# Spreading steps of the routing weights: two behind every second expert block, in two pairs of PSUM banks, in place of one behind each block

## The reference, cut to what matters

```python
ids = e1 * PEER_N_KEYS + e2                       # 128 experts per token (8 heads x top 16)
wts = jax.nn.softmax(top_v, axis=-1)
...
ue = jnp.take(u, idx, axis=0)
act = jnp.einsum('td,tkd->tk', hx, ue)
coef = w * jax.nn.gelu(act, approximate=False)
ve = jnp.take(v, idx, axis=0)
return jnp.einsum('tk,tkd->td', coef, ve)
```

## Time and profile before

| what | value |
|---|---|
| time, median of 3 runs | 1499.66 us (1498.52 to 1499.95) |
| time of the profiled execution | 1499.56 us |
| its span | 1497.7 us |
| TensorE busy | 1476.2 us (99%) |
| VectorE busy | 1243.0 us (83%) |
| ScalarE busy | 577.9 us (39%) |
| GpSimd busy | 438.9 us (29%) |
| DMA, mean over the span | 289 GB/s |

### The profile page before, as it was taken

One profiled execution on the slowest core, in us unless ns is written; L12 is line 12 of the kernel. 1 busy time (PEld: TensorE's weight loads), 2 busy tenths in 40 slices (PEclk: granted clock), 3 DMA queues, 4 the chain that ended last, 5 costly groups with the idle time before them and its releaser, 6 DMA issues.

```text
span 1497.7 us, 21867 instructions
## 1 busy us (share of the span) xinstructions
PE 1476.2 (99%) x8153; PEld 1302.1 (87%) x8153; DVE 1243.0 (83%) x2368; ACT 577.9 (39%) x869; POOL 438.9 (29%) x373
## 2 busy tenths in 40 slices
PE   8999999999999999999999999999999999999998
PEld 4788878788999999999999999988888888888886
DVE  5687868776899997999999945698888888888886
ACT  4422244522333333444444443343333333333333
POOL 1120100010578986432222202222222222222210
PEclk9999999999999999999999999999999999999999
DMA  9772423234469896799999999999999999999983
GB/s 379 271 264 87 141 96 113 60 88 148 142 210 307 293 304 220 259 347 360 365 378 360 372 321 362 382 406 359 378 355 377 371 388 378 388 358 373 366 318 131
DMA packets 152215, 433.50 MB, mean 289 GB/s; under 512 B 13520, under 2 KB 46544, under 8 KB 150224
## 3 DMA queue, kind: packets, MB, share of 16 engines
q1 hardware_dynamic: 76352, 203.91, 37.4%
q0 software_dynamic: 42048, 153.11, 28.2%
q10 hardware_dynamic: 33744, 75.64, 13.5%
HBM read 378.08 MB, written 54.53 MB: 289 GB/s over the span
## 4 chain that ended last, share of the span: by engine, by line
PE 74%; DVE 19%; DMA 4%; issue 1%; ACT 1%; POOL 0%; SPq 0%; DVEq 0%; ACTq 0%
PE ps L1733 23%; PE ps L1735 22%; PE ps L1734 22%; PE ps L2137 3%; DVE rows L1530 2%; DMA g_dram<-g_buf 2%; DVE ps L1562 1%; DMA part_w<-w_ada 1%; DVE ps L1566 1%; DVE picks L1568 1%; PE ps L2077 1%; DMA ada_w<-w_ada 1%; DVE tv L1496 1%; DVE tv L1499 1%; DVE ti L1500 1%
## 5 line engine op out<-in xcount | busy, mean ns | idle before, releaser
L1733 PE MATMUL ps<-hT_hi,ws_hi 128*128 128x384 f32 (+1 forms) x976 | 341.3, 350 | 2.8 <-POOL ws_lo L652 1.6
L1735 PE MATMUL ps<-hT_hi,ws_lo 128*128 128x384 f32 (+1 forms) x976 | 335.3, 344 | 0.0
L1734 PE MATMUL ps<-hT_lo,ws_hi 128*128 128x384 f32 (+1 forms) x976 | 335.1, 343 | 0.0
L1733 PE MATMUL ps<-vs_hi,coef_hi 128*128 128x512 f32 x768 | 298.8, 389 | 1.7 <-DVE coef_lo L1692 1.7
L1735 PE MATMUL ps<-vs_hi,coef_lo 128*128 128x512 f32 x768 | 298.8, 389 | 0.0
L1734 PE MATMUL ps<-vs_lo,coef_hi 128*128 128x512 f32 x768 | 298.8, 389 | 0.0
L994 ACT ACTIVATE vs_hi<-blk_raw 128x1024 fp32r<-128x1024 f32 x128 | 135.7, 1060 | 284.7 <-PE ps L1735 282.6
L660 POOL DMA_INDIRECT rows<-u_nat,ids x128 | 143.7, 1122 | 299.9 <-DVE sp_act L1530 292.0
L660 POOL DMA_INDIRECT rows<-v_nat,ids x128 | 127.1, 993 | 332.9 <-DVE ps L1650 298.5
L1689 DVE TENSOR_TENSOR vs_lo<-blk_raw,vs_hi 128x1024 fp32r<-128x1024 f32 x128 | 156.7, 1224 | 67.3 <-ACT vs_hi L994 65.4
L940 ACT ACTIVATE ws_hi<-blk_raw 128x1024 fp32r<-128x1024 f32 x102 | 108.1, 1060 | 239.7 <-PE ps L1735 225.4
(11 more groups left out here) (322 smaller groups left out, 2226.7 us busy)
## 6 DMA issues: line engine op xcount, KB each, us to landing
blk_raw<-u_t SPq DMA_DIRECT2D x128, 512.0 KB
blk_raw<-v_nat SPq DMA_DIRECT2D x128, 512.0 KB
g_dram<-g_buf ACTq DMA_DIRECT2D x128, 192.0 KB
w_dram<-w_stage SPq DMA_DIRECT2D x48, 512.0 KB
grp_g<-g_dram ACTq DMA_DIRECT2D x15, 1536.0 KB
grp_w<-w_dram ACTq DMA_DIRECT2D x15, 1536.0 KB
part_w<-w_ada POOLq DMA_DIRECT2D x24, 512.0 KB, 5.9
raw<-w_in SPq DMA_DIRECT2D x20, 512.0 KB, 5.9
```

The source lines that it names most:

```text
L1733: pe.matmul(o, lh, rh, start=start, stop=False, skip_group_check=True)
L1734: pe.matmul(o, lh, rl, start=False, stop=False, skip_group_check=True)
L1735: return pe.matmul(o, ll, rh, start=False, stop=stop, skip_group_check=True)
```

## The change

TensorE's steps come in pairs. Behind the products of every odd block of the stage it runs `spread(q, 0)` and `spread(q + 1, 1)`; behind an even block it runs none. The even step writes banks 2 and 3, the odd one banks 4 and 5. ScalarE copies both steps behind the odd block (`pair_after`). VectorE's order stays: one-hots of one step in each block. The blocks without one-hots are now the last two of each 16 (66, 67, 82, 83, 98 and 99) in place of the last of each 8, and with them move the bursts of three rows and the blocks in which SyncE issues no store. `PART_END` stays 106.

```diff
-PART_END = PART_A + STEPS // 7 * 8 + STEPS % 7
+PART_END = PART_A + STEPS // 14 * 16 + STEPS % 14
 def spreads_after(b):
-    if not PART_A <= b < PART_END or (b - PART_A) % 8 == 7:
+    if not PART_A <= b < PART_END or (b - PART_A) % 16 >= 14:
         return None
-    return (b - PART_A) // 8 * 7 + (b - PART_A) % 8
+    return (b - PART_A) // 16 * 14 + (b - PART_A) % 16
+
+def pair_after(b):
+    q = spreads_after(b)
+    return () if q is None or q % 2 == 0 else (q - 1, q)
...
-                    src = ps[:, 2 + r, :].rearrange("p (t b) -> p b t", t=4)
+                    src = ps[:, 2 + 2 * (q % 2) + r, :].rearrange("p (t b) -> p b t", t=4)
...
-                if spreads_after(b) is not None:
-                    take_w(spreads_after(b))
+                for q in pair_after(b):
+                    take_w(q)
...
-                    o = ps[:, 2 + t // 4, (t % 4) * P:(t % 4 + 1) * P]
+                    o = ps[:, 2 + 2 * p + t // 4, (t % 4) * P:(t % 4 + 1) * P]
...
-                if j % 8 < 7:
-                    spread(q, q0(j) % 2, free)
+                if j % 2 and j % 16 < 14:
+                    spread(q, 0, free)
+                    spread(q + 1, 1, None if free is None else free + 2)
 
             def q0(j):
-                return j // 8 * 7 + j % 8
+                return j // 16 * 14 + j % 16 - 1
 
             for j in range(16):
-                part(j, PART_A + j, q0(j), 2 * q0(j) if q0(j) else None)
+                part(j, PART_A + j, q0(j), 2 * (q0(j) - 1) if q0(j) > 0 else None)
             with pe.Fori(1, STEPS // 14) as i:
                 for j in range(16):
-                    part(j, 16 * i + (PART_A + j), 14 * i + q0(j), 28 * i + 2 * q0(j))
+                    part(j, 16 * i + (PART_A + j), 14 * i + q0(j), 28 * i + 2 * (q0(j) - 1))
             for j in range(STEPS // 14 * 16, PART_END - PART_A):
-                part(j, PART_A + j, q0(j), 2 * q0(j))
+                part(j, PART_A + j, q0(j), 2 * (q0(j) - 1))
```

## The result

| | before | after |
|---|---|---|
| median of 8 runs | 1498.62 us (1498.32 to 1499.95) | 1502.76 us (1501.86 to 1504.75) |
| ratio, 95% interval | | 1.0027 [1.0018, 1.0036] |
| profiled execution, its span | 1499.56, 1497.7 us | 1504.64, 1502.8 us |

The 8 runs of before contain the 3 of the table further up.

What follows compares the result with a forecast made beforehand. The prediction took TensorE to set the time, busy 40.00 of 40 us, with VectorE having little air. It summed -2.4 - 0.52 + 0.51 + 0.53 + 1.1 = -0.8 us on 1499.56, giving 1498.8 us, range 1497.2 to 1502.5.

Steps and rivals of the forecast that it cites:

- 24 switches: TensorE's switches from steps back to products: 24 of 48 go at 0.10 us each, -2.4 us.
- first wait, start: TensorE's wait at the first step goes, -0.52 us; late low parts at blocks 54 and 55 add +0.51 and +0.53.
- new wait at 19 pairs: VectorE's one-hots wait for the pair's first step, making TensorE 0.06 us late at 19 pairs: +1.1 us.
- three doubled bursts: Six gathered rows in two neighbouring blocks, three times: the gather is there in time, cost taken as 0.
- the one issued at 721.41: A gather on GpSimd's queue, said to land within 6.6 us, from four gathers' 2.06 MB moved between 718 and 728 us.
- T: Start of a pair of steps on TensorE, after an odd block; the forecast's times count from it.
- the fourth: Rival: at 10 us landing, doubled bursts make the low part 2 us late three times, +6, 1504.8 us; chance 0.08.
- harmless by itself: VectorE's idle time at the new wait, forecast some 20 times at about 0.8 us.
- TensorE's 0.97 us per step: Price of one step with its switch on TensorE: 16 matmuls 0.87 us, switch back to products 0.10.
- the stretch without one: TensorE around block 59, which has no step: 9.29 us against 5.13, so a bare block takes 4.16 us.
- the loads explain the switch: TensorE's 0.10 us switch put down to a 188 ns fp32r weight load with only a 0.054 us matmul to hide under.
- The stall: TensorE late at `products(b+1)` behind a pair: second matmul at T + 6.24 against T + 6.18, 0.06 us.

Runs made afterwards that it cites:

- e3: Kernel before with single steps, no pairing; only the blocks without a step moved together, giving bursts of six rows: 1499.48 us, ratio 1.0.
- a2: The changed kernel run again unedited, as the mark for its group: 1502.28 us, ratio 1.0025 against the kernel before.
- e5: Changed kernel with VectorE's row ahead of the one-hots in one block of 16, the last before a burst: 1498.47 us, ratio 1.0003.
- e8b: Changed kernel with three quarters of the `w_stage` stores taken out of the stage; part of the result wrong: 1531.57 us in one run, stage 261.16 us.
- e6: e2 with one gathered row each taken from blocks 52 and 53 and put to 106 and 110: 1495.19 us, ratio 0.9973 against the kernel before.
- e1: Changed kernel with one row in place of three in each burst's second block, six rows moved behind block 114: 1500.43 us, ratio 1.0009.
- e2: Changed kernel with VectorE's row put ahead of the one-hots in even blocks: 1497.52 us, ratio 0.999 against the kernel before.
- e7: Changed kernel with both steps of a pair in banks 2 and 3, the odd one waiting for ScalarE's copy: 1576.91 us in one run.
- e6b: e6 run again unedited, as the mark for its group: 1494.64 us, ratio 0.9968 against the kernel before.

## Why the prediction was wrong, by its own steps

| term | forecast | measured |
|---|---|---|
| 24 switches | -2.4 | 24 x 0.08 = -1.9 |
| first wait, start | -0.52 + 1.04 | -0.52 + 1.03 |
| new wait at 19 pairs | +1.1 | 19 x 0.03 = +0.57 |
| three doubled bursts | 0 | +3.95 |
| sum in the stage | -0.8 | about +3.1 |

**The step that failed** is "so the one issued at 721.41 landed within 6.6 us. That leaves 1.0 us, and another 0.4 before TensorE feels it. I take 0; it begins to cost beyond 8.0 us." The times on both sides of the landing were right. With T at 677.75, the gather starts at T - 0.52 (forecast - 0.46), and the row would have been ready to start at 684.94, T + 7.19 (forecast 7.15). The landing was wrong: 8.57 to 9.37 us from start to use, past the 8.0 named. I had divided the bytes of ten microseconds by four gathers and read that as a time for one. The landings that the profiles of e3 and a2 list, 8.5 and 9.4 us in the median of the stage, are above 8.0 as well. Bytes per microsecond are a rate and say nothing of when one of several transfers under way at the same time lands. The earlier trace rows bound no landing time, since no row there waits for a gather: in the stage of the kernel before the shortest time from a gather's start to its use is 17.1 us (623.26 to 640.39). The rival that said this, the fourth, was the right one and had 0.08. Its price of 6 us was for 10 us of landing; at the measured ones it is 3.95 (1.00, 1.21 and 1.74 at the three bursts). Both e5 and e8b show the mechanism: an earlier gather, or fewer stores beside it, removes most of the delays. Why, at nearly the same load, one gather lands after 7.3 us and another after 9.7 stays open (e6).

**What it missed beside that** is that the burst cost only together with the new wait (e3 against after). I had costed the two apart: the wait as "harmless by itself", the burst by its gather. The wait makes VectorE late against ScalarE: it paused for a high part 35 times in e3 (19.9 us from 600 to 885 us), and once in after. Without these pauses the sixth row asks for its gather 7.71 us after its start and not 8.67, and VectorE has less time left before TensorE needs the next low part. In before the bursts are apart and the same distance is 17.1 us.

**Right:** TensorE's 0.97 us per step and the stretch without one; the start, 11.22 us for the first period against 10.19 free (e6), as worked out; the new wait's size and count, and that it hardly reaches TensorE at the pairs. In e1 the first period was 10.70, so the start's 1.03 is not the same in every profile.

**Off in size:** the switch saves 0.080 us a pair, not 0.10, read as the 10.267 us of two single steps less e2's 10.187. Some of it is in the steps themselves: the 32 matmuls take 679.52 - 677.75 = 1.77 us in place of 1.75. That the loads explain the switch was argued and isn't shown: the 188 ns loads of the earlier trace rows stand at product matmuls 173 ns apart, so the duration in such a row isn't the time that the array is held. The stall is 0.030 in place of 0.06, where the prediction's own terms, 1.12 + 2.41 + 1.14 + 1.23, add up to 5.90 and not 5.91, which gives 0.05. Each of the two puts the sum off by 0.5 us.

**From +3.1 to +4.1.** In the profiles the stage is 2.9 us longer and the mixing's start 0.7 shorter (TensorE's wait for `coef_lo` is 1.0 in place of 1.7), together +2.2. The medians differ by 4.1, and by 3.4 in a2. Part of the gap is which execution was profiled: that of before took 1499.56 us, 0.9 above its median. The dip of the clock at 200 us is not the rest. Of all executions on record of the two kernels in which the mean granted clock was 0.999 or more, the 11 of the changed kernel have a median of 1502.26 and the 48 of the kernel before 1498.55, 3.7 apart. What makes up the last microsecond stays open.

## What to carry to other kernels

A wait that costs nothing where it stands still moves the engine behind it; add it to every margin further down that engine's queue before you call it harmless. A landing time is read at an instruction that waits for the transfer, not from a rate of bytes; here it varied by 2 us and more at nearly the same rate. And where an engine's order is written by hand, put work that depends on nothing new ahead of the instruction that waits: e2 did so and turned +4 us into -1; the wait itself stayed.

## What the runs showed of the hardware

- A gather of 512 KB landed 8.5 us after its issue in the median of the stage of e3 and 9.4 us in a2. The single ones read here took 7.3 (e2) to 10.4 us (e5), with the DMA engines at a share of 0.98 (348 GB/s) and of 1.00 (363 GB/s) meanwhile. At 0.94 one was there within 7.6 us (e8b, 320 GB/s) and one after 9.6 (e6b, 323 GB/s).
- After 13 of 24 waits of TensorE of some 2.3 us each the granted clock was 0.50 for about 3 us (e7), after the other 11 it stayed at 1.00. After a wait of 0.2 us (after, 680 to 720) and one of 1.57 us (before, 580 to 600) it was 1.00.
- GpSimd's issue of a gather takes 0.94 us alone. It takes 1.68 where it starts while VectorE writes a low part (677.23 in after: it ends at 678.91, VectorE's operation at 678.09). In the stage the median went from 0.94 to 1.68 us; the new wait shifts VectorE's order against GpSimd's. That the one holds up the other is only read from these rows; no run tested it.
